# The up projection of the second block: three 256-column matmuls per tile in place of a 512- and a 256-column one

## What is computed

```
h = rmsnorm_2(x, norm_mlp[l])
u = jax.nn.relu(jnp.einsum('bsd,df->bsf', h, w_up[l]))        # D_FF_2 = 8192
x = x + jnp.einsum('bsf,fd->bsd', u * u, w_down[l])
```

## Time and profile before

| | us |
|---|---|
| median of 3 runs | 3662.02 (3661.04 to 3667.2) |
| profiled execution, whole | 3660.28 |
| profiled execution, span from first to last instruction | 3658.3 |

### The profile page before, as it was taken

One profiled execution on the slowest core, in us unless ns is written; L12 is line 12 of the kernel. 1 busy time (PEld: TensorE's weight loads), 2 busy tenths in 40 slices (PEclk: granted clock), 3 DMA queues, 4 the chain that ended last, 5 costly groups with the idle time before them and its releaser, 6 DMA issues.

```text
span 3658.3 us, 59737 instructions
## 1 busy us (share of the span) xinstructions
PE 3334.6 (91%) x25150; PEld 3133.6 (86%) x25150; DVE 2344.0 (64%) x2598; ACT 1432.7 (39%) x1408; POOL 157.8 (4%) x292
## 2 busy tenths in 40 slices
PE   3487997999999979989999999998898999999997
PEld 3486887999999978777899999998887889999997
DVE  6777678756656566567666656566566755656565
ACT  1133333344444433344444444444344534443443
POOL 2111111100000000012000000000001000000000
PEclk9998998999999989999999999999999999999999
DMA  9677766755555544334455555554333455555553
GB/s 321 226 268 275 254 233 255 263 196 193 191 190 194 195 138 139 110 110 139 161 192 187 191 188 191 188 191 154 113 110 121 153 173 186 192 186 193 185 193 115
DMA packets 320587, 681.63 MB, mean 186 GB/s; under 512 B 14609, under 2 KB 21461, under 8 KB 320005
## 3 DMA queue, kind: packets, MB, share of 16 engines
q1 hardware_dynamic: 283440, 560.11, 46.2%
q0 software_dynamic: 31232, 109.07, 8.6%
q10 hardware_dynamic: 5780, 10.53, 0.8%
HBM read 677.47 MB, written 7.94 MB: 187 GB/s over the span
## 4 chain that ended last, share of the span: by engine, by line
PE 80%; DVE 10%; DMA 5%; issue 3%; ACT 2%; ACTq 0%; POOLq 0%; POOL 0%; DVEq 0%; SPq 0%
PE G L598 47%; PE Dn L598 31%; DMA ada_raw<-in_w_ada 3%; DVE w_lo L1063 2%; DVE ada_acc L1164 2%; DMA raw<-in_w_in 2%; PE Dn L601 1%; DVE sq L1099 1%; ACT w_hi L1792 1%; DVE negmax L1391 0%; DVE xT L1418 0%; DVE xT L1629 0%; DVE h_hl L1637 0%; DMA raw<-in_w_ffn_up 0%; ACT zT L1927 0%
## 5 line engine op out<-in xcount | busy, mean ns | idle before, releaser
L598 PE MATMUL G<-h_hl,w_hi 128*128 128x256 f32 (+1 forms) x9472 | 2072.8, 310 | 66.4 <-DVE w_lo L1063 25.0
L598 PEld LDWEIGHTS G<-h_hl,w_hi 128*128 128x128 f32 x9472 | 1550.5, 193 | 174.9 <-issue 32.8
L598 PE MATMUL G<-h_hl,w_lo 128*128 128x256 f32 x5760 | 1630.0, 283 | 0.0
L1063 DVE TENSOR_TENSOR w_lo<-raw,w_hi 128x2048 fp32r<-128x2048 f32 (+2 forms) x536 | 1219.1, 2275 | 600.3 <-ACT w_hi L1792 597.6
L1792 ACT CAST w_hi<-raw 128x2048 fp32r<-128x2048 f32 (+2 forms) x536 | 1016.6, 1898 | 1383.1 <-DMA raw<-in_w_up 387.4
L598 PEld LDWEIGHTS G<-h_hl,w_lo 128*128 128x128 f32 x5760 | 1105.9, 192 | 0.0
L598 PE MATMUL Dn<-act_hi,w_hi 128*128 128x256 f32 x2752 | 762.4, 277 | 7.3 <-DVE act_lo L1500 7.3
L598 PE MATMUL Dn<-act_lo,w_hi 128*128 128x256 f32 x2752 | 762.2, 277 | 0.0
L598 PE MATMUL Dn<-act_hi,w_lo 128*128 128x256 f32 x2752 | 762.0, 277 | 0.0
L598 PEld LDWEIGHTS Dn<-act_hi,w_hi 128*128 128x128 f32 x2752 | 518.3, 188 | 9.3 <-DVE act_lo L1500 7.9
L598 PEld LDWEIGHTS Dn<-act_hi,w_lo 128*128 128x128 f32 x2752 | 518.4, 188 | 0.0
(11 more groups left out here) (193 smaller groups left out, 1607.7 us busy)
## 6 DMA issues: line engine op xcount, KB each, us to landing
raw<-in_w_up SPq DMA_DIRECT2D x128, 1024.0 KB, 5.4
raw<-in_w_down SPq DMA_DIRECT2D x128, 1024.0 KB, 5.0
ada_raw<-in_w_ada POOLq DMA_DIRECT2D x192, 512.0 KB, 5.7
raw<-in_w_in SPq DMA_DIRECT2D x88, 1024.0 KB, 5.3
raw<-in_w_ffn_gate SPq DMA_DIRECT2D x44, 1024.0 KB, 5.0
raw<-in_w_ffn_up SPq DMA_DIRECT2D x44, 1024.0 KB, 5.0
raw<-in_w_ffn_down SPq DMA_DIRECT2D x44, 1024.0 KB, 5.0
raw<-in_w_o SPq DMA_DIRECT2D x32, 1024.0 KB, 5.0
```

What stands on the lines that cost most here:

```text
L598: return nc.tensor.matmul(o, lhsT, rhs, start=start, stop=stop, skip_group_check=True)
L1063: v.tensor_tensor(w_lo[j][:, 0:m], raw[j][:, 0:PIECE_K * n], w_hi[j][:, 0:m], ALU.subtract).then_inc(lo_done, 1)
```

## The change

The up projection uses `piece` with `G[0]` alone. `piece_pair`, the view `GP`, the step `ff_half` on ACT and the addition on DVE are gone; DVE's relu reads `G[0]` in PSUM and frees it. ACT's square waits for that release. `h_hi` and `h_lo` are two buffers at the addresses that the two halves of `h_hl` had, and the accumulators `G[0]`, `G[1]` are allocated one by one, in the same banks. Up groups of the second block no longer wait for `g_free[1]`. Weights, their pieces, slots and order are as before.

```
-            def piece_pair(quad, j, out, rhs, kts, first, last):
-                ...
-                for kk in range(PIECE_K):
-                    for f in range(4):
-                        c = P * f
-                        mm(out[:, f, :, :], hi[:, kk, c:c + P], rhs[:, :, kts + kk, :], first and kk == 0, False)
-                        i = mm(out[:, f, 0, :], lo[:, kk, c:c + P], rhs[:, 0, kts + kk, :], False, last and kk == PIECE_K - 1)
-                i.then_inc(pe_done, 1)
...
                             if j == 0:
                                 pe.wait_ge(g_free[0], gb[0] + (i + 10))
-                                if first:
-                                    pe.wait_ge(g_free[1], gb[1] + 10)
-                            piece_pair(quad, j, GP, h_hl, 4 * UP_ORDER[j], j == 0, j == 3)
+                            piece(quad, j, G[0], h_hi, h_lo, 4 * UP_ORDER[j], j == 0, j == 3)
...
-                    def ff_relu(i):
-                        dve.wait_ge(half_out, l * FF2_GROUPS + 1 + i)
-                        v.tensor_tensor(stage_p[:, :, :], stage_p[:, :, :], GP[:, :, 0, :], ALU.add).then_inc(g_free[0], 1)
-                        dve.wait_ge(g_free[0], gb[0] + 11 + i)
-                        v.scalar_tensor_tensor(out=stage_p[:, :, :], in0=stage_p[:, :, :], scalar=0.0,
+                    def ff_relu(i, pieces):
+                        dve.wait_ge(pe_done, pieces)
+                        dve.wait_ge(a_lo, an + i)
+                        v.scalar_tensor_tensor(out=stage_p[:, :, :], in0=G[0][:, :, :], scalar=0.0,
                                                in1=rstd[:, :].unsqueeze(1).broadcast_to([P, 4, T]),
-                                               op0=ALU.max, op1=ALU.mult).then_inc(relu_done, 1)
+                                               op0=ALU.max, op1=ALU.mult).then_inc(g_free[0], 1)
...
-                    def ff_half(i, pieces):
-                        act.wait_ge(pe_done, pieces)
-                        act.wait_ge(a_lo, an + i)
-                        s.copy(stage_p[:, :, :], GP[:, :, 1, :]).then_inc(half_out, 1)
                     def ff_square(i):
-                        act.wait_ge(relu_done, l * FF2_GROUPS + 1 + i)
+                        act.wait_ge(g_free[0], gb[0] + i + 11)
```

More of the change, by code:

```diff
@@ L240, in two_stage_kernel @@
         rs_v = sb("rs_v", [P, 16])
-        h_hl = sb("h_hl", [P, 2, KT, T], F32R)
-        h_hi, h_lo = h_hl[:, 0, :, :], h_hl[:, 1, :, :]
+        h_hi = sb("h_hi", [P, KT, T], F32R)
+        h_lo = sb("h_lo", [P, KT, T], F32R)
         rs_y = sb("rs_y", [P, 16])
@@ L325, in two_stage_kernel @@
         o_tok = x_tok
-        G_all = ctx.enter_context(nc.psum_tensor("G", [P, 8, T], F32))
-        G = [G_all[:, 0:4, :], G_all[:, 4:8, :]]
-        GP = G_all[:, :, :].rearrange("p (f h) t -> p f h t", h=2)
+        G = [ctx.enter_context(nc.psum_tensor(f"G{i}", [P, 4, T], F32)) for i in range(2)]
         Dn = [ctx.enter_context(nc.psum_tensor(f"Dn{i}", [P, 4, T], F32)) for i in range(2)]
@@ L399, in two_stage_kernel @@
         ff_p = sem("hidden_product_done")
-        half_out = sem("hidden_second_half_out")
-        relu_done = sem("hidden_relu_done")
         a_hi = sem("hidden_hi")
@@ L617, in piece @@
                             i.then_inc(misc_w, 1)
-                i.then_inc(pe_done, 1)
-            def piece_pair(quad, j, out, rhs, kts, first, last):
-                pe.wait_ge(lo_done, quad * 4 + (j + 1))
-                hi = w_hi[j][:, 0:PIECE_K * PIECE_N].rearrange("p (k n) -> p k n", k=PIECE_K)
-                lo = w_lo[j][:, 0:PIECE_K * PIECE_N].rearrange("p (k n) -> p k n", k=PIECE_K)
-                for kk in range(PIECE_K):
-                    for f in range(4):
-                        c = P * f
-                        mm(out[:, f, :, :], hi[:, kk, c:c + P], rhs[:, :, kts + kk, :], first and kk == 0, False)
-                        i = mm(out[:, f, 0, :], lo[:, kk, c:c + P], rhs[:, 0, kts + kk, :], False, last and kk == PIECE_K - 1)
                 i.then_inc(pe_done, 1)
@@ L1715, in _ @@
                         if n == 4:
-                            ff_relu(0)
+                            ff_relu(0, lp + 52)
                         if n == 7:
@@ L1726, in body2 @@
                             if n == 0:
-                                ff_relu(k + 1)
+                                ff_relu(k + 1, pc)
                             if 1 <= n <= 4:
@@ L1739, in _ @@
                         if n == 0:
-                            ff_relu(FF2_GROUPS - 1)
+                            ff_relu(FF2_GROUPS - 1, pc)
                         if n == 4:
@@ L2190, in _ @@
                         run_hooks(48 + n)
-                        if n == 4:
-                            ff_half(0, lp + 52)
                         if n == 6:
@@ L2199, in _ @@
                             hi(lq + k * 2 + (14 + (n + 1) // 4), (n + 1) % 4)
-                            if n == 0:
-                                ff_half(k + 1, lp + k * 8 + 56)
                             if n == 3:
@@ L2209, in _ @@
                             hi(lq + (14 + 2 * (FF2_GROUPS - 2) + (n + 1) // 4), (n + 1) % 4)
-                        if n == 0:
-                            ff_half(FF2_GROUPS - 1, pc)
                         if n == 2:
```

## The result

| | median, us | lowest to highest | runs |
|---|---|---|---|
| before | 3664.61 | 3661.04 to 3667.58 | 4 |
| changed | 3637.66 | 3634.67 to 3642.62 | 4 |

The ratio is 0.9928, with a 95% interval of 0.9911 to 0.9945: 27.0 us less, where 27.6 was forecast. The time itself is 3.3 us above the 3634.4 that was forecast and inside the range of 3630 to 3640; 2.6 of the 3.3 are in the median of before, 3664.61 over these four executions where the forecast had started from 3662.02. A later comparison of the same two kernels gave 0.9913 (0.9894 to 0.9932).

What follows compares the result with a forecast made beforehand. TensorE's matmul spacing was taken as the bound. Gains of 23.9 (loop), 1.6 (up 1), 2.1 (handover), 0 (up group 0) and 0 (clock) sum to 27.6 us, giving 3634.4 us, range 3630 to 3640.

Steps and rivals of the forecast that it cites:

- Spacing by form: Second block's loop rounds: narrow matmuls at 113.3 ns take a round from 44.37 to 43.52 us, 23.9 us over 28 rounds.
- Up 1: Up group 1 of each layer, ahead of the loop: 22.06 us in place of 22.87, counted as 1.6 us over both layers.
- The handover: From up group 0 to up group 1: TensorE's stall falls from 2.34 to about 1.3 us, 2.1 us over both layers.
- The start of up 0: Before piece 48: 1.51 us of idle goes but DVE's chain swallows it, idle before the sum of squares 3.3 us; gain 0.
- The clock: Low-clock stretches in up 1 and piece 50: +0.8 and -0.8 us, together 0, bounds +1.6 and -3.2.
- Beside TensorE: ACT's copies and DVE's additions beside down groups: removal gains nothing, though busy time falls 39 us on DVE, 32 on ACT.
- No gain: Second block's up pieces keep the after-break spacing, 5.65 us for 48 matmuls; only 2.1 us gained, 3660 us; chance 5%.
- slower: The 128 up pieces: a third start per tile costs more than the wide one loses, 3687 us at worst; chance 4%.
- the third rival: In the loop, late transfers or w_lo, or more low-clock stretches, give back half the gain: 3646 us; chance 5%.
- The rule of the Trainium skill: Up tiles: columns over 2.4 GHz plus 2.5 ns per matmul, pair 325 ns, triple 327.5, so 5.1 us slower; prediction disbelieved it.

Runs made afterwards that it cites:

- the wait put back: The changed kernel with the wait on g_free[1] restored before up group 0 of each layer; 3636.25 us, 0.9925 of the kernel before.
- two and two: The kernel before with up matmuls reordered within a k tile: two 512-column ones, then two 256-column ones, and so on; 3644.57 us.
- both wide: The kernel before with both matmuls of each up tile 512 columns wide, the second adding the product of the low parts; 3881.36 us.

## Why the prediction was right

- **Spacing by form.** The step was to read 113.3 ns for narrow matmuls from the first block and the down groups, 353.1 for the pair, and to hold that form decides and place doesn't. The loop lost 11.95 us in each layer, 23.9 us together as forecast. The kernel with three narrow matmuls in the accumulators of before shows that it is the form.
- **Up 1.** Forecast 22.06 us, measured 22.05 and 22.04. The exactness is in part luck: the 22.06 was read from layer 1 of before, and the same four pieces after a wait took 22.47 us in layer 2, a value that up 1 does take with the wait put back (22.45):

```profile
2885.02 22.47 PE G L598 x192
```

- **The handover.** Forecast 1.3 us, measured 1.30. All of it comes from the copy that is gone (1.02 us and its handing over); it counts only where two up groups touch.
- **The start of up 0.** That it is swallowed was right: from the end of piece 47 to the sum of squares it is 15.11 us after (1781.09 to 1796.20) and 15.12 before. The size of the idle was wrong: 4.27 us, not 3.3. I had taken the `w_lo` at 1777.76 for piece 49's, and it is piece 50's; piece 49's stands before the last addition to the residual, so piece 49 didn't wait at all. Nothing was lost by it but the estimate of the idle, and with it the low clock behind the idle was judged too mildly.
- **The clock.** Forecast 0 in sum, with +0.8 for a low stretch that goes and -0.8 for longer idle. In the profile the first was +1.5 (up 1 of layer 2 has none, 22.04 for 24.39 us), and the second -1.5, so that the 0 came out by luck. The +1.5 isn't shown to be an effect of the change: of the twelve up 1 groups that start after the long handover of 2.34 us, in the six profiles that have it, only this one had a low stretch. The prediction names the stretch in piece 50 for layer 1 alone; layer 2 of before has one as well, from 2923.3 to 2926.7 us. The -1.5 comes from the stretch from the sum of squares to the end of up 0: layer 1 took 14.86 for 13.96 us there and layer 2 14.53 for 13.95. The windows show the low stretch, twice as long as that in the earlier trace rows and begun in the idle, before the first small matmul:

```profile
1792.00:1794.80 2.80, 0.00 (x0) 0.00 (x0) 2.80 (x2) 1.90 (x1) 0.00 (x0) 1.00 0.52 140
1794.80:1801.50 6.70, 5.30 (x25) 5.33 (x26) 5.05 (x18) 1.90 (x1) 0.00 (x0) 0.51 0.26 100
```

- **Beside TensorE.** DVE's busy time fell by 33.5 us and ACT's by 28.6, less than the 39 and 32 that I had taken from durations, since instructions that follow each other closely overlap by 0.1 us and busy time counts that once. Over the 14 rounds of layer 1 DVE's durations fell by 16.95 us, and of its overlaps 2.31 us went with them. Neither moved the end.
- **The rivals.** "No gain" and "slower" needed 117.7 ns or more per matmul throughout. Such a spacing does exist, but only in the first pieces after a break: piece 51 took 5.67 us for its 48 matmuls in both layers, while an up group in the loop is at 113.3 ns throughout. Nothing came late at the quicker pace; the third rival fell with the loop's 609.28 us.
- **The rule of the Trainium skill** ("TensorE: Matmul & The Clock Gate", section "Back-to-back issue gap") had the sign wrong here. It puts one matmul of 512 columns at 215.8 ns and of 256 at 109.2; here they are 231.2 and 113.3. It is 4 ns short for the narrow one and 15 ns for the wide one, which is why counting instructions by it favours the pair. The section itself gives the rule for an isolated matmul, and says that at 512 columns a stream of weight loads and matmuls is faster than it, at about 131 ns; in this kernel's stream, where every matmul has its weight load, the wide one is slower than the rule.

## What to carry to other kernels

Where TensorE is the only name on the chain, compare start-to-start times of the forms at hand, at a full clock and away from breaks, before assuming that fewer and wider matmuls are cheaper: here three of 256 columns beat one of 512 and one of 256 by 13 ns a tile. Work removed from other engines counts only where TensorE waits for it, and an earlier start only if nothing later waits on the same chain. Moving one small sum behind the next piece and one group into the other accumulator took away the idle, the low clock after it and the handover, for a further 13 us, half as much as the change itself (3622.61 us for 3635.74, side by side).

## What the runs showed that I had not expected

- fp32r matmuls of 512 columns follow each other at 231.2 ns; of 256 columns at 113.3. In the low stretch of before a pair, 768 columns, starts every 0.64 us, which is one column per cycle of 1.2 GHz. By that measure at 2.4 GHz the wide one is 17.9 ns above its columns and the narrow one 6.6. In strict alternation a pair costs 8.6 ns more than the two spacings together, and two and two 1.3 more.
- A narrow piece after hooks or a wait takes 5.65 to 5.86 us for 48 matmuls at full clock, in the changed kernel too (5.67 us for piece 51); a few take 5.46. It can last into the next pieces: up 1 took 22.19 us where it followed piece 51 without a wait, and after the handover 22.05 us in the changed kernel and 22.45 with the wait put back. What it is that lags isn't shown.
- The idle before the sum of squares of the second feed-forward part was followed by a low clock almost each time. After 4.27 us it had begun in the idle itself in three of four cases (2 to 3 us after TensorE's last matmul), for 6.8 us; in the fourth it began behind the sum, for 3.4 us. After 2.1 to 2.5 us of idle it began within piece 50, for 3.4 us, in 13 of 14 cases, and in one (layer 1 with the wait put back) not at all. Without idle there (both wide, and the kernels with the later sum) it didn't fall.
